# Scaling attention probabilities with a diagonal matrix instead of scaling the attention output, in a four-layer fp32 kernel

## The reference, cut to what matters

```python
for l in range(2):
    h = rmsnorm(x, norm_mix[l])
    proj = h @ w_in[l]                      # 1024 -> 3476, split into 17 parts
    qk = silu(causal_conv(concat(m_q, m_k), conv_qk[l]))
    y_m = mlstm(qk..., m_v, m_o, m_i, m_f, m_norm[l])   # 4 heads of 128
    y_b = moba(b_q, b_k, b_v, ...)                      # 4 heads of 64
    y_n = nsa(n_q, n_kc, n_vc, n_ks, n_vs, n_kw, n_vw, n_g, ...)  # 4 heads of 64
    mix = concat(y_m, y_b, y_n)             # 512 + 256 + 256
    x = x + mix @ w_out[l]
    x = x + square(relu(rmsnorm(x, norm_ffn[l]) @ w_ff1[l])) @ w_ff2[l]
# mlstm returns sigmoid(o_pre) * rmsnorm(h)
# nsa returns gates[0]*o_cmp + gates[1]*o_selected + gates[2]*o_window
```

## Time and profile before

| | before |
|---|---|
| median of 3 runs | 1140.25 us (1138.59 to 1141.14) |
| profiled execution, its own time | 1139.48 us |
| its span | 1137.7 us |
| PE busy | 1089.9 us, 96% |
| PEld busy | 952.3 us, 84% |
| DVE busy | 717.2 us, 63% |
| ACT busy | 623.3 us, 55% |
| POOL busy | 57.5 us, 5% |
| mean granted TensorE clock | 0.987 |

### The profile page before, as it was taken

The page is one execution under the profiler, slowest core; times in us unless marked ns, Lnnn a source line. Parts: engine busy times, 40 slices in busy tenths (PEclk is TensorE's granted clock), DMA queues, the critical chain, the costliest instruction groups (busy, mean ns, idle before and its releaser), DMA issues.

```text
span 1137.7 us, 17472 instructions
## 1 busy us (share of the span) xinstructions
PE 1089.9 (96%) x6848; PEld 952.3 (84%) x6848; DVE 717.2 (63%) x1260; ACT 623.3 (55%) x983; POOL 57.5 (5%) x75
## 2 busy tenths in 40 slices
PE   8989989999999989899999999999999899999997
PEld 6878779899888977779998987798988677989885
DVE  4799577555557898576555556774445657844555
ACT  4555746445545555745454445665657447666562
POOL 0010000000000000100000000004000000040000
PEclk8999999999999999999999999999999999999999
DMA  8753336655666542346656655554453455444441
GB/s 272 236 162 94 111 111 209 198 186 186 185 190 206 181 130 87 118 128 206 187 187 183 195 187 185 168 152 131 120 158 118 129 161 168 149 130 131 147 130 56
DMA packets 89087, 181.17 MB, mean 159 GB/s; under 512 B 8797, under 2 KB 19933, under 8 KB 89005
## 3 DMA queue, kind: packets, MB, share of 16 engines
q1 hardware_dynamic: 87565, 175.79, 49.8%
q10 hardware_dynamic: 1440, 4.26, 1.1%
HBM read 178.98 MB, written 1.05 MB: 158 GB/s over the span
## 4 chain that ended last, share of the span: by engine, by line
PE 73%; DVE 14%; ACT 5%; issue 5%; DMA 2%; POOL 1%; SPq 0%; DVEq 0%; POOLq 0%; ACTq 0%
PE bank L778 21%; PE bank L780 21%; PE bank L779 21%; DVE w_lo L1623 4%; ACT w_hi L1252 2%; DMA raw<-in_w_in 2%; PE bank L855 2%; PE bank L906 1%; DVE xn L1895 1%; DVE vecs L1632 1%; PE bank L953 1%; PE bank L1191 1%; PE bank L962 1%; PE bank L963 1%; PE bank L929 1%
## 5 line engine op out<-in xcount | busy, mean ns | idle before, releaser
L1623 DVE TENSOR_TENSOR w_lo<-raw,w_hi 128x1024 fp32r<-128x1024 f32 (+1 forms) x320 | 389.4, 1220 | 309.2 <-ACT w_hi L1252 305.0
L1252 ACT ACTIVATE w_hi<-raw 128x1024 fp32r<-128x1024 f32 (+1 forms) x320 | 334.8, 1051 | 243.2 <-PE bank L780 219.6
L778 PE MATMUL bank<-h_hi,w_hi 128*128 128x256 f32 x896 | 257.4, 287 | 4.2 <-ACT hid_parts L1391 4.1
L780 PE MATMUL bank<-h_hi,w_lo 128*128 128x256 f32 x896 | 253.3, 283 | 0.0
L779 PE MATMUL bank<-h_lo,w_hi 128*128 128x256 f32 x896 | 253.3, 283 | 0.0
L778 PE MATMUL bank<-w_hi,h_hi 128*128 128x512 f32 (+1 forms) x448 | 182.6, 407 | 5.4 <-DVE h_lo L1642 4.8
L778 PEld LDWEIGHTS bank<-h_hi,w_hi 128*128 128x128 f32 x896 | 170.9, 191 | 8.2 <-issue 7.0
L780 PE MATMUL bank<-w_hi,h_lo 128*128 128x512 f32 (+1 forms) x448 | 176.4, 394 | 0.0
L779 PE MATMUL bank<-w_lo,h_hi 128*128 128x512 f32 (+1 forms) x448 | 176.2, 393 | 0.0
L779 PEld LDWEIGHTS bank<-h_lo,w_hi 128*128 128x128 f32 x896 | 171.0, 191 | 0.5
L780 PEld LDWEIGHTS bank<-h_hi,w_lo 128*128 128x128 f32 x896 | 170.9, 191 | 0.0
(11 more groups left out here) (290 smaller groups left out, 1329.2 us busy)
## 6 DMA issues: line engine op xcount, KB each, us to landing
raw<-in_w_in SPq DMA_DIRECT2D x144, 512.0 KB, 3.8
raw<-in_w_ff SPq DMA_DIRECT2D x128, 512.0 KB, 4.0
raw<-in_w_out SPq DMA_DIRECT2D x40, 512.0 KB, 3.2
raw<-in_w_in SPq DMA_DIRECT2D x8, 404.0 KB, 5.8
xn<-in_cmp_w SPq DMA_DIRECT2D x8, 256.0 KB, 5.0
x_sb<-in_x SPq DMA_DIRECT2D x2, 512.0 KB, 7.5
mix<-in_cmp_w SPq DMA_DIRECT2D x4, 256.0 KB, 4.7
gain<-in_cmp_w SPq DMA_DIRECT2D x4, 256.0 KB, 5.5
```

The lines of the kernel that those rows point to most:

```text
L778: pe.matmul(out_ap, s_hi, m_hi, start=start, stop=False, **kw)
L780: return pe.matmul(out_ap, s_lo, m_hi, start=False, stop=stop, **kw)
L1252: act.activation(slot(w_hi, u), slot(raw, u), ACT.Copy).then_inc(hi_ready, 1)
L1623: dve.tensor_tensor(slot(w_lo, u), slot(raw, u), slot(w_hi, u).bitcast(F32), ALU.subtract)\
```

## The change

Three things are changed in the layers of the first kind.

1. The attention heads. Before the turn, DVE makes for each pair of heads a tile of four 128x128 diagonal matrices (identity times the inverse row sums, times the gate; `scale_rows`, step D, two places after S). T is now three full fp32 matmuls with a block of probabilities as weights and a diagonal moving, which turn and scale at once. V has the values as weights (64 columns) and the turned probabilities moving (256 and 128 columns), for a pair of heads into the two halves of a bank's partitions. The output then lies feature by row and is split straight into `mixT_hi` and `mixT_lo` (`mix_rows`); gates, branches and the compressed branch are summed in the bank. `epilogue1`, the addition of `cmp_o` and the `mix_turn` steps for these columns go. Heads run in six pairs with places `start = [13, 15, 18, 20, 22, 24]` and lags E 1, D 2, T 3 and 4, V 5.
2. The tile order: the output gate is the sixth tile, the recurrence's values are the last. So the two sigmoids stand at p = 23, where the silu of the convolution is.
3. Steps moved: `cmp` one place earlier, `cmp_kT` from 19 to 20, `cmp_s` and `cmp_soft` from 20 to 22, `cmp_o` in place 26, `m_values` one or two places later, `mlstm_end` in two halves of two heads (four 128x128 operations each instead of two of 128x1024), `ff_params` from 19 to 29. Copies of a flag on DVE are gone, clearing of tiles went from DVE to POOL.

```diff
-PROJ1 = [4, 5, 6, 0, 1, 2, 3]
+PROJ1 = [4, 5, 6, 0, 1, 3, 2]
...
-        start = [13, 14, 15, 16] + list(range(18, 26))
+        start = [13, 15, 18, 20, 22, 24]
         CONV_AT = {16: (0,), 17: (1, 2), 18: (3,), 20: (4,), 21: (5, 6), 22: (7,)}
         def heads1(p):
-            for stage, lag in (("V", 4), ("T", 2), ("E", 1), ("S", 0)):
+            name = ("att1", l)
+            for c, first in enumerate(start):
+                if first + (4 if c == 5 else 5) == p:
+                    if c in (0, 2):
+                        use((*name, "O", c // 2), 7)
+                    if c in (1, 5):
+                        done((*name, "O", c // 4))
+                    step(*name, "V", 2 * c)
+                    if c in (1, 5):
+                        step("mix_rows", l, c // 4)
+            for h in range(12):
+                c = h // 2
+                if start[c] + 3 + (h % 2 if c < 5 else 0) == p:
+                    use((*name, "T", h), 4 if h == 11 else 6)
+                    step(*name, "T", h)
+            for c, first in enumerate(start):
+                if first + 2 == p:
+                    step(*name, "D", 2 * c)
+            for stage, lag in (("E", 1), ("S", 0)):
                 for h in range(12):
-                    if stage == "V" and h > 8:
-                        lag = 3
-                    first = start[h - h % 2] if stage in ("E", "S") else start[h]
-                    if first + lag == p:
-                        head_steps(("att1", l), h, stage, 4)
+                    if start[h // 2] + lag == p:
+                        head_steps(name, h, stage, None)
...
-                if p == 14:
+                if p == 13:
                     use(("hidden_parts", l), 0)
                     step("cmp", l, 0)
-                if p == 15:
+                if p == 14:
                     step("cmp", l, 1)
                     done(("hidden_parts", l))
                     step("hidden_parts", l)
                 if p == 16:
-                    single(3, "hidden", l)
+                    single(2, "hidden", l)
                 if p == 17:
                     single(3, "turn", l, 2)
-                    single(3, "turn", l, 3)
+                    single(2, "turn", l, 3)
                 if p == 18:
                     single(2, "cmp_kv", l)
                     single(3, "turn", l, 5)
-                if p == 19:
-                    single(3, "cmp_kT", l)
-                    if l == 0:
-                        step("ff_params")
                 if p == 20:
+                    single(1, "cmp_kT", l)
+                if p == 22:
                     single(0, "cmp_s", l, 0)
                     single(1, "cmp_s", l, 1)
                     step("cmp_soft", l)
-                if p == 21:
-                    single(0, "mix_turn", 0, l, 2)
-                if p == 24:
+                if p == 25:
                     single(3, "cmp_pT", l)
-                if p == 25:
+                if p == 26:
+                    step("cmp_o", l)
                     m_scores(0, 2)
-                if p == 26:
-                    single(3, "cmp_o", l)
-                    m_scores(1, 2)
-                    m_values(0, 5)
                 if p == 27:
-                    m_scores(2, 4)
-                    m_values(1, 5)
+                    m_scores(1, 3)
...
-                m_scores(3, 4)
+                m_values(0, 5)
+                m_scores(2, 6)
+                m_values(1, 4)
+            if p == 29:
+                m_scores(3, 6)
                 m_values(2, 5)
-            if p == 29:
-                single(6, "mix_turn", 0, l, 3)
-                m_values(3, 5)
-                step("mlstm_end", l, 0)
+                step("mlstm_end", l, 0, 0)
+                m_values(3, 4)
+                step("mlstm_end", l, 0, 1)
+                if l == 0:
+                    step("ff_params")
             if p == 30:
-                step("mlstm_end", l, 1)
+                step("mlstm_end", l, 1, 0)
+                single(7, "mix_turn", 0, l, 0)
+                step("mlstm_end", l, 1, 1)
             if p == 31:
-                single(7, "mix_turn", 0, l, 0)
...
+            def value_pair(l, h):
+                for c in range(2):
+                    drained(pe, ("att1", l, "T", h + c))
+                group = ("att1", l, "O", h // 4 if h < 4 else 1)
+                first, last = h in (0, 4), h in (2, 10)
+                ps = open_bank(group) if first else bank[bank_of[group]]
+                lo = T * (h // 2 if h < 4 else (h - 4) // 4)
+                for i in range(NT):
+                    for c in range(2):
+                        v = heads_of("att1", l)[h + c][3](i)
+                        weight = probsT_at("att1", h + c)
+                        mm = pe.matmul(ps[HD * c:HD * c + HD, lo + i * P:lo + T], v, weight[:, i * T:i * T + T - i * P],
+                                       start=first and i == 0, stop=last and i == 1, skip_group_check=True)
+                if last:
+                    close(mm, group)
-                if stage in ("E", "C"):
+                if stage in ("E", "C", "D"):
...
+                        pe.wait_ge(scale_ready, 6 * l + h // 2 + 1)
                     ps = open_bank((*name, "T", h))
                     for b in range(3):
-                        mm = pe.transpose(ps[:, b * P:(b + 1) * P], probs[:, h % 3, b * P:(b + 1) * P], ident)
+                        block_ = probs_at(kind, h)[:, b * P:(b + 1) * P]
+                        if kind == "att1":
+                            mm = pe.matmul(ps[:, b * P:(b + 1) * P], block_, row_scale[h // 2 % 2][:, 2 * (h % 2) + (b + 1) // 2, :],
+                                           start=True, stop=True)
+                        else:
+                            mm = pe.transpose(ps[:, b * P:(b + 1) * P], block_, ident)
                     close(mm, (*name, "T", h))
+                elif kind == "att1":
+                    value_pair(l, h)
                 else:
                     g, r = divmod(h, GROUPS[kind])
                     last = kind == "diff" or r == GROUPS[kind] - 1
...
-                def epilogue1(g):
-                    name = ("att1", l, "O", g)
-                    ps = src(name)
-                    ov = ps[:, :].rearrange("p (h i d) -> p h i d", h=4, i=NT)
-                    link(dve.reciprocal(row_inv, row_sum[:, g % 2]))
-                    lo = 512 if g == 0 else 768
-                    dst = mix[:, :, lo:lo + 256].rearrange("p i (h d) -> p h i d", d=HD)
-                    if g:
-                        tt(row_inv, row_inv, n_gate[:, :, 4 * g:4 * g + 4].rearrange("p i h -> p h i"), ALU.mult)
-                    f = row_inv.unsqueeze(3).broadcast_to([P, 4, NT, HD])
-                    if g < 2:
-                        free(dve.tensor_tensor(dst, ov, f, ALU.mult), name)
-                        if g == 0:
-                            signal(mix_ready)
-                        return
-                    t = o_tmp[:, :].rearrange("p (h i d) -> p h i d", h=4, i=NT)
-                    free(dve.tensor_tensor(t, ov, f, ALU.mult), name)
-                    dve.tensor_tensor(dst, dst, t, ALU.add).then_inc(mix_ready, 1)
+                def scale_rows(h):
+                    dve.wait_ge(exp_ready, nth_head("att1", l, h + 1))
+                    inv = row_inv[:, 0:2, :]
+                    link(dve.reciprocal(inv, row_sum[:, h // 2 % 2, 0:2, :]))
+                    if h >= 4:
+                        n, branch = divmod(h - 4, 4)
+                        at_gate = 4 * (1 + branch // 2) + 2 * n
+                        tt(inv, inv, n_gate[:, :, at_gate:at_gate + 2].rearrange("p i h -> p h i"), ALU.mult)
+                    dve.tensor_tensor(row_scale[h // 2 % 2], ident.unsqueeze(1).broadcast_to([P, 4, P]),
+                                      inv.rearrange("p h i -> p (h i)").unsqueeze(2).broadcast_to([P, 4, P]), ALU.mult)\
+                        .then_inc(scale_ready, 1)
...
                     elif kind == "mlstm_end":
-                        inv = m_den[:, :, 4:8]
-                        dve.wait_ge(h_rstd_ready, l + 1)
-                        tt(inv, inv, h_rs, ALU.mult)
+                        r = slice(2 * s[2], 2 * s[2] + 2)
+                        inv = m_den[:, :, 4 + 2 * s[2]:6 + 2 * s[2]]
+                        dve.wait_ge(m_rstd_ready, 2 * l + s[2] + 1)
+                        tt(inv, inv, h_rs[:, :, r], ALU.mult)
                         dve.wait_ge(o_gained, NT * (l + 1))
-                        hn = h_num[:, :, :, 0:P]
-                        tt(hn, hn, inv.unsqueeze(3).broadcast_to([P, NT, MH, P]), ALU.mult)
-                        dve.tensor_tensor(mix[:, :, 0:512].rearrange("p i (h d) -> p i h d", d=P), hn, o_gate, ALU.mult)\
-                            .then_inc(mix_ready, 1)
+                        for h in (2 * s[2], 2 * s[2] + 1):
+                            for i in range(NT):
```

(9 more changed lines are left out.)

144 lines of the change are left out of this document (75 added, 69 removed).

## The result

| | before | after |
|---|---|---|
| median | 1139.42 us (4 runs) | 1157.39 us (1154.97 to 1158.84, 4 runs) |
| profiled execution, its span | 1139.48, 1137.7 us | 1157.37, 1155.6 us |
| PE / DVE / ACT busy | 1089.9 / 717.2 / 623.3 us | 1099.3 / 722.1 / 623.7 us |
| mean granted TensorE clock | 0.987 | 0.980 |

The account below looks back on a forecast made before the run. TensorE sets the end of the heads' stretch, with DVE nearly as busy, so work ahead of TensorE's waits comes late. Two layers at +8.1, -1.2 and clock +3.5 make +18.5 on 1139.5: 1158 us, range 1141 to 1164.

Parts of the forecast that it names:

- TensorE's own work comes to about nothing: Both layers: T +5.5 us, V -4.5, fewer turns -2; sum within 1 us of nothing, between -4 and +5.
- rival F: V's two halves don't overlap: +5.5 us, mostly inside waits, +2 to the forecast; within the forecast's 0.64.
- First T waits 3.1 for the diagonals: First pair of heads: DVE's diagonals done at about 76.7 us, TensorE there at 73.5, so T waits 3.1.
- Rival A: TensorE's clock keeps its level through the longer waits: 1155 us; within the forecast's 0.64.
- Third pair waits 2.8: T at p = 21: diagonals done at 103.1 us, TensorE there at 100.3; it waits 2.8, giving back earlier gains.
- ACT's block: 3.6 and 4.9: p = 22 to 24: ACT's late copies make T(7) wait 3.6 us and V of the fourth pair 4.9.
- rival C: ACT's block is longer, each of four table switches costing 0.5 to 1.5 of 1.28 us more: 1166 us; chance 0.08.
- Unit at 165.2: End of the first layer's projection: the unit that began at 157.04 us begins at 165.2, +8.1 us a layer.
- End of the recurrence: 0.75 and 3.2: TensorE's waits at the recurrence's end: 0.75 and 3.2 us, before 1.32 and 1.05; the last chain between 2 and 5.
- The wait at 38.52 goes: First layer alone: the 1.25 us wait for DVE goes, as casts and clearing ahead of it move; -1.2 us.
- Clock +3.5: More stretches of low TensorE clock behind the longer waits, both layers: +3.5 us, between 0 and +9.
- Rival D: DVE has the diagonals ready before T, ACT's copies aren't held, old waits go and none replace them: 1128 us; chance 0.10.

Follow-up runs that it names:

- first_d: Changed kernel with the first pair's diagonals made ahead of DVE's two additions into the convolution's tile at p = 15; 1157.59 us, ratio 1.0159 to the kernel before.
- filler: Changed kernel with extra matmuls, their result overwritten, in TensorE's three long waits of each layer; 1155.63 us, ratio 1.0142 to the kernel before.
- gate_last: Changed kernel with the tile order of before (output gate last, sigmoids at p = 27); 1152.12 us, ratio 1.0111 to the kernel before.
- mend: Changed kernel with the statistics of the recurrence's second pair of heads at p = 29 instead of 30, ff_params at 31; 1153.28 us, ratio 1.0128.
- small_diag: Changed kernel with the diagonals' 128x512 multiplication cut to 128x8, leaving out the probabilities' scaling; 1151.31 us, ratio 1.0118 to the kernel before.
- combo_d: Changed kernel with the old tile order, the recurrence's scores, values and statistics early, and three units' low parts a layer on POOL; 1154.45 us, ratio 1.0152.

## Why the prediction was right, point by point

- *TensorE's own work comes to about nothing.* Right: T 0.66 as forecast, V 0.80 against 0.85. The halves of a V pair do run beside each other; rival F is out. One reading behind it was wrong: the 32 rows of `cmp` in 1.08 us are 16 matmuls, two rows for each fp32 one as in the `x2` of the 0.22, so 0.068 each and not 0.034. That parts run beside each other holds with either number.
- *First T waits 3.1 for the diagonals.* 3.15. Both sides were 1 us earlier than I had them: D done at 75.7, not 76.7, TensorE there at 72.6, not 73.5. Rival A is out too: behind this wait the clock fell to 0.51.
- *Third pair waits 2.8.* This step failed as a wait. D is done at 102.0 and T is there at 102.09, with no wait. What I had missed is that the clock stayed low from 76 to 82 and used up the same time. first_d and filler show that the two can be exchanged: with the clock held, waits for DVE take its place. DVE's time at that place was right to 1.1 us (102.0 against 103.1), so the sum was.
- *Fourth pair 0.9.* 0.70, and 1.03 that I did not see, for a bank that the compressed scores leave late.
- *ACT's block: 3.6 and 4.9.* 2.49 and 4.72, all four loads at 1.28 each with the work right behind; rival C is out. gate_last puts a price on the exchange of the tiles: 5.3 us for both layers.
- *Unit at 165.2.* 165.02, but these are not the same sum. The 165.2 has neither the 1.2 us saved at 38.52 nor the added low clock, and the 165.02 has both. The waits were over-counted, and the missing clock hid it.
- *End of the recurrence: 0.75 and 3.2.* 0.31 and 2.80; I took it for the length of a chain, and mend, where the last turn doesn't wait, shows that it was an order on DVE that one can change.
- *The wait at 38.52 goes.* Half of it: 0.68 us are left at the like place (36.92). The heads' scores began 1.05 us earlier (58.73 against 59.78), but in this execution the clock was also 0.97 over the first 54 us and not 0.94. In first_d and small_diag, at 0.94, they began at 59.09 and 59.87, so the edit itself brought between nothing and 0.7 us.
- *Clock +3.5.* 8.3 by the mean. The term was too small by 5 and the waits too large by as much: together 18 us, as forecast. The total is better than its parts, since time lost to the clock ahead of a wait for DVE shortens the wait. The prediction added the two as if they were independent, so its agreement to 1 us is partly luck; that DVE would set the time, which keeps their sum, was its sound part.
- *Rival D, DVE has room:* decided by D being ready before TensorE. At the first T it was not, and small_diag shows that the point was not near: even without the multiplication the first T waits 2.6. At the third pair it was, by 0.1 us, but only since TensorE itself was late by the low clock.

## What to carry to other kernels

Where two engines are both busy for some nine tenths of a stretch (TensorE 57.3 and DVE 59.3 of 64 us here), follow the second one's order as closely as the first's. What shortened TensorE's waits alone gained nothing here (first_d), and what was on DVE counted nearly in full (5 to 6 of 6.5 us), wherever the wait then showed. Before exchanging two pieces of work, look at what stands between them and at the activation tables that each leaves loaded. And a wait and the low clock behind it are one cost with the wait that comes after: price them as one chain on the engine that is late.

## What the runs showed of the hardware

- Matmuls on two halves of the array's columns (values 64 wide as weights, 256 and 128 columns moving) run beside each other: 0.80 us for four fp32 matmuls of together 768 columns, where a 128-column one on the whole array is 0.22 (0.22 x 6 = 1.32 one after the other).
- DVE operations without an input from a bank that began beside a product or difference on POOL were held until it had ended: 0.18 became 2.25 us, 1.22 became 3.37 (combo_d). Those with an input from a bank were not: 0.28 and 0.42 as ever. POOL is held too. In the changed kernel two products of 128x512 take POOL 3.52 us (118.68) beside a low part of DVE that takes 2.29; in combo_d, with only a short operation on a bank beside them, the two take 2.51 (146.57).
- Extra matmuls in a wait kept the full clock behind it (1.00 instead of 0.51 over 76 to 82 us, mean 0.988 instead of 0.980), but where DVE sets the pace only 1.8 us of the 9 came out, which is not clear of noise (filler).
